# A fused transformer kernel: rows, sink and weight splits of its three attentions stand elsewhere

## The reference

```python
# first block: heads of 64, 8 of them; its two gates and the pooling branch run beside the attention
merged = sigmoid(g_attn) * (attn @ w_branch_attn) + sigmoid(g_pool) * (pool @ w_branch_pool)
x = x + gate1 * (merged @ w_out)

# second attention (swa), 16 heads: the sink is one more logit that has no value
m = jnp.maximum(jnp.max(s, axis=-1), sink_f)
p = jnp.exp(s - m[..., None])
denom = jnp.sum(p, axis=-1) + jnp.exp(sink_f - m)
p = p / denom[..., None]

# third attention (fox), 16 heads: q, k, v are 1024 wide each, plus a forget term in the logits
s = jnp.einsum('bqhd,bkhd->bhqk', qb, k) + Fq[..., None] - F[:, :, None, :]
p = jax.nn.softmax(jnp.where(kpos[None, :] <= qpos[:, None], s, -jnp.inf), axis=-1)
```

## Time and profile before

| | |
|---|---|
| profiled execution | 1485.89 us, span 1484.1 us, mean granted TensorE clock 0.983 |
| TensorE busy | 1405.3 us, 95% of the span |
| VectorE, ScalarE, GpSimd busy | 73%, 49%, 9% |
| a split, L972 | 215 times, mean 2287 ns |
| an operation of an ada piece, L930 | mean 751 ns |
| an ada piece's DMA | 512 KB, median 6.0 us from issue to landing |
| first attention with its branches | about 40 to 210 us |
| second attention, its steps | 646 to 714 us |
| third attention, its steps | 1161 to 1276 us |

### The profile page before, as it was taken

How to read it: one execution, slowest core, us unless ns; L and a number is a source line. 1 busy time by engine, 2 the same in 40 slices (tenths; PEclk the granted TensorE clock), 3 DMA queues, 4 the chain that set the end, 5 groups by cost and what they waited for, 6 DMA issues and landing times.

```text
span 1484.1 us, 18511 instructions
## 1 busy us (share of the span) xinstructions
PE 1405.3 (95%) x7259; PEld 1162.7 (78%) x7259; DVE 1085.7 (73%) x1523; ACT 730.7 (49%) x1033; POOL 140.7 (9%) x199
## 2 busy tenths in 40 slices
PE   2899999999999999998999999999999989999998
PEld 1688988999878888765788887788878755788886
DVE  5878977898979997766578887788886435566444
ACT  3653464444554433776643336443447555553332
POOL 1111001111012220000011110111110000000000
PEclk9899999999999999999999999999999997999999
DMA  9876757788679997350598886788845430475552
GB/s 352 280 223 233 241 170 255 248 279 261 234 253 351 335 345 274 114 170 1 163 311 301 300 300 213 252 303 300 293 156 178 167 113 1 142 255 182 183 183 76
DMA packets 189289, 333.63 MB, mean 225 GB/s; under 512 B 8850, under 2 KB 132478, under 8 KB 188180
## 3 DMA queue, kind: packets, MB, share of 16 engines
q1 hardware_dynamic: 161392, 236.02, 47.0%
q0 software_dynamic: 27232, 96.21, 19.3%
q10 hardware_dynamic: 580, 0.23, 0.1%
HBM read 331.27 MB, written 1.15 MB: 224 GB/s over the span
## 4 chain that ended last, share of the span: by engine, by line
PE 82%; DVE 9%; ACT 5%; issue 2%; DMA 2%; SPq 0%; ACTq 0%; DVEq 0%
PE bank L1483 10%; PE bank L1485 10%; PE bank L1484 10%; PE bank L1446 8%; PE bank L1448 8%; PE bank L1447 7%; PE bank L1378 4%; PE bank L1379 4%; PE bank L1380 4%; DVE lo L972 4%; PE bank L1611 2%; PE bank L1613 2%; PE bank L1612 2%; PE bank L1684 2%; DMA V<-in_ada_w 1%
## 5 line engine op out<-in xcount | busy, mean ns | idle before, releaser
L972 DVE TENSOR_TENSOR lo<-raw,hi 128x2048 fp32r<-128x2048 f32 x215 | 491.0, 2287 | 77.0 <-ACT hi L536 76.4
L536 ACT ACTIVATE hi<-raw 128x2048 fp32r<-128x2048 f32 x215 | 405.6, 1910 | 19.3 <-DMA raw<-in_w_out 12.8
L1483 PE MATMUL bank<-hi,h_hi 128*128 128x512 f32 x704 | 278.1, 395 | 3.6 <-DVE lo L972 2.0
L1485 PE MATMUL bank<-hi,h_lo 128*128 128x512 f32 x704 | 274.5, 390 | 0.0
L1484 PE MATMUL bank<-lo,h_hi 128*128 128x512 f32 x704 | 274.2, 389 | 0.0
L1446 PE MATMUL bank<-hi,o_hi 128*128 128x512 f32 x504 | 204.3, 405 | 11.6 <-DVE lo L972 9.5
L1448 PE MATMUL bank<-hi,o_lo 128*128 128x512 f32 x504 | 197.4, 392 | 0.0
L1447 PE MATMUL bank<-lo,o_hi 128*128 128x512 f32 x504 | 196.9, 391 | 0.0
L648 ACT ACTIVATE KT<-bank 128x256 f32<-128x256 f32 x88 | 33.8, 384 | 312.9 <-PE bank L1485 312.8
L1483 PEld LDWEIGHTS bank<-hi,h_hi 128*128 128x128 f32 x704 | 132.2, 188 | 33.8 <-DVE lo L972 3.9
L1485 PEld LDWEIGHTS bank<-hi,h_lo 128*128 128x128 f32 x704 | 132.1, 188 | 28.1
(11 more groups left out here) (215 smaller groups left out, 2001.5 us busy)
## 6 DMA issues: line engine op xcount, KB each, us to landing
raw<-in_ffn_w SPq DMA_DIRECT2D x176, 512.0 KB, 5.3
ada<-in_ada_w POOLq DMA_DIRECT2D x100, 512.0 KB, 6.0
raw<-in_ffn_w SPq DMA_DIRECT2D x44, 1024.0 KB, 6.5
V<-in_ada_w POOLq DMA_DIRECT2D x76, 512.0 KB, 5.9
raw<-in_w_up SPq DMA_DIRECT2D x22, 1024.0 KB, 5.2
raw<-in_w_in SPq DMA_DIRECT2D x16, 1024.0 KB, 7.7
raw<-in_fox_w_in SPq DMA_DIRECT2D x12, 1024.0 KB, 5.2
raw<-in_w_down SPq DMA_DIRECT2D x11, 1024.0 KB, 6.5
```

What stands on the lines that cost most here:

```text
L536: nc.scalar.activation(hi[:, n % NS, :], raw[:, n % NS, :], ACT.Copy).then_inc(hi_ready, 1)
L972: nc.vector.tensor_tensor(lo[:, n % NS, :], raw[:, n % NS, :], hi[:, n % NS, :].bitcast(F32), ALU.subtract).then_inc(lo_ready, 1)
L1483: mm(bank[:, :], xk_hi, wh[:, i, :], start=k == 0, stop=False, skip_group_check=True)
L1485: ins = mm(bank[:, :], xk_lo, wh[:, i, :], start=False, stop=k == KD - 1, skip_group_check=True)
```

## The change

Four things. In the first attention one ada piece and the split of unit 12 move into step 10 of the heads on VectorE, unit 13's high part into step 9 on ScalarE, and the turns r start one unit later. In the second attention all rows of the third block stand ahead of the heads, the two last norms too (on ScalarE and VectorE), and the turns of these blocks come in steps 1 and 2; later splits move to later steps. The sink is now a column beside the logits: GpSimd writes it into the probability buffer, the exponentials run over 129 and 257 columns and sum it, and the extra exponential and the addition go. In the third attention the rows are dealt out differently over nine steps, the last block goes to bank S, and in both attentions a step's rows stand between its logits and its turn.

```diff
-ROWS_FROM = {"swa": 8, "fox": 16}
-ROWS_STEP = {"swa": (3, 3, 2), "fox": (8,) * 6}
+ROWS_FROM = {"swa": 16, "fox": 16}
+ROWS_STEP = {"swa": (), "fox": (7, 7, 6, 6, 8, 6, 0, 4, 4)}
...
-        for u0 in (2, 7, 8, 9, 10, 11, 12, 12, 13, 14, 15, 16, 16, 17, 18, 18):
+        for u0 in (2, 7, 8, 9, 10, 11, 12, 13, 14, 15, 16, 16, 17, 18, 18):
...
+            def sinks(s):
+                pool.wait_ge(nsink_done, 1)
+                pool.wait_ge(xt_done, 4 * s + 4)
+                for h in range(HEADS[KINDS[s]]):
+                    n = HEAD0[s] + h
+                    if n >= 3:
+                        pool.wait_ge(tr_done, n - 2)
+                    nc.gpsimd.tensor_copy(P_of[n % 3][:, P:P + 2 + T:T + 1],
+                                          nsink[:, h:h + 1].to_broadcast([P, 2])).then_inc(sink_set, 1)
...
             by_distance(1, 16)
+            load_pieces(4)
+            sinks(3)
             load_pieces(6)
...
                 if KINDS[s] == "swa":
-                    ins = nc.scalar.activation(st[:, 6:8], st[:, 2:4], ACT.Exp, bias=sink[:, h:h + 1])
-                ins.then_inc(exp_done, 1)
+                    act.wait_ge(sink_set, h + 1)
+                    first, second = slice(0, P + 1), slice(P + 1, P + 2 + T)
...
# ScalarE, first attention
-                        if t in (1, 3, 5, 7):
+                        if t in (1, 3, 5, 7, 9):
                             split_through(s, 9 + (t - 1) // 2)
# ScalarE, second attention
                     block_square(s, 4)
+                    block_root(s, 4)
+                    block_square(s, 5)
+                    block_root(s, 5)
                     for t in range(HEADS[kind] + 3):
                         attention_step(s, t)
-                        if t == 2:
-                            block_square(s, 5)
-                        elif t == 3:
-                            block_roots(s, 4)
-                        elif t in (5, 6):
-                            block_evict(s, t - 1)
-                        if t in (1, 3, 5, 7):
-                            split_through(s, 7 + (t - 1) // 2)
-                        elif t == 17:
-                            split_through(s, 11)
+                        if t in (1, 2):
+                            block_evict(s, t + 3)
+                        if t in (7, 10, 12, 14, 17):
+                            split_through(s, 7 + (7, 10, 12, 14, 17).index(t))
# VectorE, first attention
-                        pieces(int(t in (1, 3, 5, 7, 9)))
-                        if t in (0, 2, 4, 6, 8):
+                        pieces(int(t in (1, 3, 5, 7, 9, 10)))
+                        if t in (0, 2, 4, 6, 8, 10):
                             split_through(s, 7 + t // 2)
                     dve.wait_ge(p_ready, 2)
                     for r in range(8):
-                        split_through(s, 10 + r)
+                        split_through(s, 11 + r)
# VectorE, second attention: block_sums and block_norm of 4 and 5 ahead of the heads, then
-                        if t in (1, 2, 4, 6, 8):
-                            split_through(s, 6 + t // 2)
+                        if t in (5, 8, 11, 13, 15):
+                            split_through(s, 6 + (5, 8, 11, 13, 15).index(t))
# TensorE
-                if h in (SWITCH, SWITCH + 1) and KINDS[s] == "fox":
-                    pe.wait_ge(v_ready, V0[s] + 3 + h - SWITCH)
+                if h == SWITCH and KINDS[s] == "fox":
+                    pe.wait_ge(v_ready, V0[s] + 3)
...
                 if t + 1 < nh:
                     logits(s, t + 1)
+                if KINDS[s] != "moba":
+                    step_rows(s, t)
                 if 0 <= t - 2 < nh:
                     turn(s, t - 2)
...
-                    step_rows(s, t)
-                    if kind == "swa" and 3 <= t < 9:
+                    if kind == "swa" and 2 <= t < 9:
                         busy(3)
```

More of the change, by code:

```diff
@@ L188, in build @@
         A, G, M, S = banks[0:4], banks[4:6], banks[6], banks[7]
-        P_of = [work[:, 384 * n:384 * n + 384] for n in range(3)]
-        PT_of = [work[:, 1152 + 384 * n:1536 + 384 * n] for n in range(2)]
+        P_of = [work[:, 386 * n:386 * n + 386] for n in range(3)]
+        PT_of = [work[:, 1158 + 384 * n:1542 + 384 * n] for n in range(2)]
+        FIRST, SECOND = slice(0, P), slice(P + 1, P + 1 + T)
         hid_hi = o_hi[:, 0:6, :].rearrange("p (a b) t -> p a b t", a=3)
@@ L298, in product_bank @@
                 return A[2 + b] if t else G[b]
-            return (G[0], G[1], M)[(2 * (b - 2) + t) % 3] if KINDS[s] == "fox" else G[t]
+            if KINDS[s] == "fox":
+                return S if (b, t) == (5, 1) else (G[0], G[1], M)[(2 * (b - 2) + t) % 3]
+            return G[t]
         def logit_bank(h):
@@ L706, in exps @@
                 act.wait_ge(am_done, n + 1)
-                nc.scalar.activation(pr[:, 0:P], pr[:, 0:P], ACT.Exp, bias=st[:, 2:3], scale=-1.0, accum_out=st[:, 4:5])
-                ins = nc.scalar.activation(pr[:, P:384], pr[:, P:384], ACT.Exp, bias=st[:, 3:4], scale=-1.0,
-                                           accum_out=st[:, 5:6])
+                first, second = FIRST, SECOND
                 if KINDS[s] == "swa":
-                    ins = nc.scalar.activation(st[:, 6:8], st[:, 2:4], ACT.Exp, bias=sink[:, h:h + 1])
-                ins.then_inc(exp_done, 1)
+                    act.wait_ge(sink_set, h + 1)
+                    first, second = slice(0, P + 1), slice(P + 1, P + 2 + T)
+                nc.scalar.activation(pr[:, first], pr[:, first], ACT.Exp, bias=st[:, 2:3], scale=-1.0, accum_out=st[:, 4:5])
+                nc.scalar.activation(pr[:, second], pr[:, second], ACT.Exp, bias=st[:, 3:4], scale=-1.0,
+                                     accum_out=st[:, 5:6]).then_inc(exp_done, 1)
             def pt_copy(s, h):
@@ L1301, in _ @@
                 elif kind == "swa":
-                    nc.vector.tensor_scalar(nsink[:, :], sink[:, :], -1.0, None, ALU.mult)
+                    nc.vector.tensor_scalar(nsink[:, :], sink[:, :], -1.0, None, ALU.mult).then_inc(nsink_done, 1)
                     block_sums(s, 0)
@@ L1312, in _ @@
                     block_norm(s, 3)
+                    block_sums(s, 4)
+                    block_norm(s, 4)
+                    block_sums(s, 5)
+                    block_norm(s, 5)
                     dve.wait_ge(bias_in, 32)
@@ L1604, in block_rows @@
                             pe.wait_ge(gate_ready, turned)
+                        elif r == 7:
+                            pe.wait_ge(bk_ready, N0[s] + len(NORMED[kind]))
                         elif before in NORMED[kind]:
                             pe.wait_ge(bn_ready, N0[s] + NORMED[kind].index(before) + 1)
-                        if r != 2 and before in VALUES[kind]:
+                        if r not in (2, 7) and before in VALUES[kind]:
                             pe.wait_ge(v_ready, V0[s] + VALUES[kind].index(before) + 1)
@@ L1664, in turn @@
                     pe.wait_ge(ptc_done, n)
+                if h == SWITCH and KINDS[s] == "fox":
+                    pe.wait_ge(v_ready, V0[s] + 4)
                 for c in range(3):
-                    ins = nc.tensor.transpose(turn_bank(h)[:, P * c:P * (c + 1)], P_of[n % 3][:, P * c:P * (c + 1)], ident[:, :])
+                    first = P * c + int(c > 0)
+                    ins = nc.tensor.transpose(turn_bank(h)[:, P * c:P * (c + 1)], P_of[n % 3][:, first:first + P], ident[:, :])
                 ins.then_inc(tr_done, 1)
@@ L1866, in _ @@
                         block_rows(s, 2, 0, 5, KD)
-                        steps(s, (5, 6))
+                        block_rows(s, 2, 1, 0, KD)
+                        steps(s, (1, 2))
                         continue
```

29 lines of the change are left out of this document (9 added, 20 removed).

## The result

The changed kernel takes 1492.54 us (median, 1488.41 to 1497.22) against 1486.12 us of the kernel before (1485.15 to 1490.9): ratio 1.004, 95% interval 1.003 to 1.0049. It is slower by 6 us where 5.5 us faster was forecast, and outside the range. The profiled execution took 1492.38 us, span 1490.6 us.

The account below looks back on a forecast made before the run. TensorE was taken as the bound, busy 95% of the span, so only its idle or lower-clock stretches could pay. Terms +3.1 - 4.0 - 4.6 = -5.5 us gave 1481 us, range 1474.5 to 1487.5.

Parts of the forecast that it names:

- Second attention: Moved rows and norms, later splits and the sink as a column: -4.0 us, between -6 and -2.
- the price of the clock: Second attention: a clock fall after the new wait costs 1.7 us, counted only in the range of -6 to -2.
- the new wait: Second attention: TensorE waits 2.4 us before head 2's logits, the first maximum being queued on VectorE behind the norm.
- the walk behind it: Second attention step by step: step 4 starts at 662.0, steps 4 to 8 take 3.0 us each, step 9 2.1; about -4.0.
- list of parts: Second attention's separate gains and costs: -6.4 - 0.5 - 0.3 - 0.8 + 2.4 + 0.9 + 0.8, stated as -2.9 us.
- First attention: Earlier splits and piece put pooling branches and large copies later on VectorE: +3.1 us, between +1 and +6.5.
- The second rival: First attention: VectorE's order costs all it can, +6.5 us; whole kernel unchanged at 1484 to 1487 us; 20%.
- the main case: All three attentions go as forecast: 1481 us, within 1477 to 1483.4; 50%.
- Third attention: Redealt rows leave waits for unit 11's split and head 8's logits, full clock before step 9: -4.6 us, between -9 and +9.
- The slower one: Third attention, steps 7 to 10: the clock is not given back, +9 us instead of -4.6, total 1494.5 us; 8%.
- Locked copies of GpSimd: Second attention's sink copies slow or locked out by weight splits: five heads each 0.8 us late, 4 us, total 1485; 8%.

Follow-up runs that it names:

- the third profile: The changed kernel profiled a third time, unaltered: 1489.58 us (one run), second attention 99.03 us with 3.4 us at the lower clock.

## Why the prediction was wrong

The sum was +3.1 - 4.0 - 4.6 = -5.5; measured are +5.4 + 3.6 - 3.2 = +5.9, and +0.85 and -0.3 from the start and the end, which the change does not touch.

**Second attention, the step that failed: the price of the clock.** "Between -6 and -2 (a clock fall after the new wait costs 1.7)" put one short fall into the tail of the range. The wait itself was right (2.4 forecast, 2.58), and so was the walk behind it: with the wait filled, step 4 begins 10.4 us after the first logits, 662.3 in the prediction's count, where it said 662.0. But the forecast let the clock hold behind an idle stretch that it had itself predicted, and gave no reason for it. It fell in all nine profiles that have the wait, four times for 3.4 us and five times for 10.2, and with the second stretch this costs 1.5 to 6.1 us, 6.1 in the profiled execution. Part of the size is chance: in the third profile, with the least low clock, the stage took 99.03 us, 0.9 less than before's, and the whole 1489.58 us, still outside the range. The other 1.5 us are in the walk: with the wait filled, steps 4 to 8 take 3.06 us each where it had 3.0, and step 9 takes 2.99 where it had 2.1, for it charged nothing for the maxima that VectorE's split of step 8 holds up (0.67 us of waiting there). With that split behind step 9, steps 9 and 10 together take 7.3 us instead of 8.7. -4.0 + 1.5 + 6.1 = +3.6. The forecast's list of parts has an error of its own: its terms add up to -3.9 and not to the -2.9 that it states, so that they agree with the walk and gave no reason for doubt.

**What the parts of it are worth.** The 3.39 and 1.30 us removed were credited to the rows and norms, and 0.8 us to the sink. The runs turn this round: the sink alone takes 1.7 us of waits, the rows' part none.

**First attention: right mechanism, two sizes off.** The forecast had the waits (none for unit 12, 1 to 2 for unit 13, some 4 for the branches, up to 2 for the copies) and the bound, VectorE's list up to the copies; the run with the fourth branch first shows that bound. The term was +3.1 and is +5.4. 0.8 of the difference is the place of the wait, which stands ahead of the eight small products and not behind them. 1.2 us is waiting of VectorE ahead of the copies: the piece behind unit 12's split landed 2.04 us late instead of 1.4, it waited 0.45 us for TensorE at 155.29, which was not foreseen, and 1.24 instead of before's 1.10 for a later piece. Some 0.3 us stay unexplained. The second rival, named with +6.5 for this stage, was closer than the main case.

**Third attention: right.** Unit 11's split 4.79 (5.0), head 8's logits after 4.16 (4.4), full clock before step 9, end of step 10 1.4 us later than said, where the clock fell once more: -3.2 instead of -4.6. Twelve profiles with the new order lie between 152.3 and 156.2 us, two with the old one at 156.6, and the lengths go with the time at the lower clock: three of the twelve would have given a gain of 0.4 to 1.2 us only. That the size came out near is in part luck.

**The rivals.** The slower one was put into the third attention (8%): a clock that is not given back although TensorE is busy. This happened, in the second attention, where it had no chance of its own. Locked copies of GpSimd exist (2.06 us for 0.19), but no head waited for one.

**Left open.** Why the low stretch lasts 3.4 or 10.2 us. It goes with where it begins relative to TensorE's restart, in nine profiles without an exception, but no run moved that start on purpose. It does not carry over to another wait: before, behind 3.39 us of waiting, the low stretch began 1.1 us after the restart and lasted 3.4 us. Why the waits of 0.68 and 0.57 us were followed by a fall in six profiles and not in two is open, too.

## What to carry to other kernels

An idle stretch of TensorE has two prices, the time itself and the clock behind it, and the second belongs into the sum and not into the tail: if a new wait like the 2.58 us here is forecast ahead of steps without rows, add the fall, and ask whether a few matmuls without use can stand in it. When work is moved to the front of a list, write down the end of everything behind it up to the last thing that TensorE needs; a wait taken away earlier only makes the next one longer. Measure stage by stage between the same two instructions before believing a total: here parts of both signs lay between stretches that agreed to 0.01 us. And take more than one profile before a difference of a few us in a stage is put down to an edit: half of one gain here was the clock's.

## What was unexpected in the hardware's behaviour

The same kernel, with identical waits, took 103.6, 100.6 and 99.0 us for one stage in three executions, by 13.6, 6.8 and 3.4 us at 1.2 GHz. TensorE was busy 10.40 of 10.40 us at the lower clock and was not given the higher one back. This alone spreads the stage by 4.6 us; the changed kernel's runs spread over 9 us. A fall of 3.4 us, beginning between 218 and 229 us at a wait of 2.2 us that every kernel has, was there in eleven profiles and absent in three, and moved that stretch by 1.6 us.
